# Expert tokens gathered for two blocks at a time, with a twentieth weight buffer in the place of x

## The reference

```python
def hierarchical_moe(hx, w_rg, b_rg, w_re, b_re, w_gate, w_up, w_down):
    g_prob = jax.nn.softmax((xt @ w_rg).astype(jnp.float32) + b_rg, axis=-1)
    g_w, g_idx = lax.top_k(g_prob, 1)
    e_logits = ...                                  # the 8 experts of that group
    e_top, e_loc = lax.top_k(e_logits, EXPERT_TOPK) # EXPERT_TOPK = 2
    e_w = jax.nn.softmax(e_top, axis=-1) * g_w
    e_id = g_idx * EXPERTS_PER_GROUP + e_loc
    ...
    def run_block(args):
        xb, e = args
        return (jax.nn.silu(xb @ w_gate[e]) * (xb @ w_up[e])) @ w_down[e]
    ...
    out = jnp.zeros((t, dm), jnp.float32).at[stok].add(y_sorted * sw[:, None])
```

## Time and profile before

| | |
|---|---|
| median of 3 runs | 1036.89 us |
| the profiled execution | 1034.23 us |
| its span, first to last instruction | 1032.4 us |
| PE busy | 1014.6 us (98%) |
| DVE busy / ACT busy | 508.4 us (49%) / 408.3 us (40%) |
| moved by DMA | 327.87 MB, mean 318 GB/s |
| queue q1 (all loads by SP), share of 16 engines' span | 81.4% |

### The profile page before, as it was taken

One profiled execution on the slowest core, in us unless ns is written; L12 is line 12 of the kernel. 1 busy time (PEld: TensorE's weight loads), 2 busy tenths in 40 slices (PEclk: granted clock), 3 DMA queues, 4 the chain that ended last, 5 costly groups with the idle time before them and its releaser, 6 DMA issues.

```text
span 1032.4 us, 13668 instructions
## 1 busy us (share of the span) xinstructions
PE 1014.6 (98%) x5584; PEld 678.4 (66%) x5584; DVE 508.4 (49%) x714; ACT 408.3 (40%) x643; POOL 21.8 (2%) x42
## 2 busy tenths in 40 slices
PE   8999999999999999999999999999999999999986
PEld 6888888888999999899887544444444344444322
DVE  5677677987987755667876412112221121111112
ACT  7734544435534454474874222222222122222213
POOL 0100000010000000100000000000000000000000
PEclk9999999999999999999999999999999999999999
DMA  9987558977788854364468899999999999999995
GB/s 329 391 291 244 166 190 286 329 253 245 251 311 296 292 194 164 99 244 164 163 224 335 325 389 422 419 421 421 422 421 420 422 421 420 421 421 422 421 420 212
DMA packets 86178, 327.87 MB, mean 318 GB/s; under 512 B 5744, under 2 KB 5904, under 8 KB 61408
## 3 DMA queue, kind: packets, MB, share of 16 engines
q1 hardware_dynamic: 84912, 323.98, 81.4%
q0 software_dynamic: 1200, 2.98, 0.9%
HBM read 325.88 MB, written 1.05 MB: 317 GB/s over the span
## 4 chain that ended last, share of the span: by engine, by line
PE 51%; DMA 5%; DVE 1%; ACT 0%; issue 0%; ACTq 0%; DVEq 0%
PE bank L1028 19%; PE bank L1053 9%; PE bank L1072 3%; PE bank L995 3%; DMA es<-in_w_expert_down 3%; DMA raw<-in_w_expert_gate_up 3%; PE bank L587 2%; PE bank L590 2%; PE bank L1038 2%; PE bank L593 2%; PE bank L555 1%; PE bank L558 1%; PE bank L561 1%; PE bank L1009 1%; PE bank L1011 1%; PE bank L768 1%
## 5 line engine op out<-in xcount | busy, mean ns | idle before, releaser
L1635 DVE TENSOR_TENSOR wlo<-raw,whi 128x2048 fp32r<-128x2048 f32 x87 | 199.1, 2290 | 85.7 <-ACT whi L1130 85.4
L1130 ACT ACTIVATE whi<-raw 128x2048 fp32r<-128x2048 f32 x87 | 166.0, 1913 | 95.4 <-PE bank L561 36.6
L2277 DVE SCALAR_TENSOR_TENSOR YS<-bank,wsl,gate2q 128x512 f32<-128x512 f32 x32 | 24.1, 752 | 213.8 <-PE bank L1053 213.8
L1028 PE MATMUL bank<-es,XT 128*64 128x512 f32 x488 | 112.6, 596 | 1.0 <-DMA es<-in_w_expert_gate_up 0.7
L555 PE MATMUL bank<-whi,hh 128*128 128x512 f32 x224 | 88.1, 393 | 1.2 <-ACT whi L1137 1.2
L558 PE MATMUL bank<-wlo,hh 128*128 128x512 f32 x224 | 87.3, 390 | 0.2 <-DVE wlo L1644 0.2
L561 PE MATMUL bank<-whi,hl 128*128 128x512 f32 x224 | 87.3, 390 | 0.0
L1028 PE MATMUL bank<-raw,XT 128*64 128x512 f32 x336 | 77.6, 596 | 0.4 <-DMA raw<-in_w_expert_gate_up 0.4
L1028 PEld LDWEIGHTS bank<-es,XT 128*64 128x64 f32 x488 | 33.5, 137 | 66.4 <-issue 66.1
L1624 DVE SCALAR_TENSOR_TENSOR ada_acc<-raw,silu_c,ada_acc 128x512 f32<-128x512 f32 x96 | 72.0, 750 | 2.5
L590 PE MATMUL bank<-fl,whi 128*128 128x256 f32 x256 | 72.5, 283 | 0.4 <-DVE fl L1822 0.4
(11 more groups left out here) (387 smaller groups left out, 1807.9 us busy)
## 6 DMA issues: line engine op xcount, KB each, us to landing
es<-in_w_expert_gate_up SPq DMA_DIRECT2D x61, 1024.0 KB, 24.5
raw<-in_w_expert_gate_up SPq DMA_DIRECT2D x42, 1024.0 KB, 21.1
raw<-in_w_in SPq DMA_DIRECT2D x41, 1024.0 KB, 6.0
raw<-in_w_ff SPq DMA_DIRECT2D x32, 1024.0 KB, 5.3
es<-in_w_expert_down SPq DMA_DIRECT2D x30, 1024.0 KB, 22.2
raw<-in_w_ada SPq DMA_DIRECT2D x24, 1024.0 KB, 5.7
raw<-in_w_expert_down SPq DMA_DIRECT2D x19, 1024.0 KB, 24.8
e_wlo<-in_w_expert_gate_up SPq DMA_DIRECT2D x13, 1024.0 KB, 23.0
```

The costliest lines, as they stand in the source:

```text
L1028: m = e.matmul(b[64 * w:64 * w + 64, :], K.XT[j // 4 % 2][:, k, j % 4, :], K.weights(i)[:, o:o + 512], start=k == 0, stop=k == 7)
L1130: e.activation(whi[n % RING][:, :], raw[h.raw][:, :], ACT.Copy).then_inc(S["hi"], 1)
L1635: e.tensor_tensor(wlo[n % RING][:, :], raw[h.raw][:, :], whi[n % RING][:, :].bitcast(F32), ALU.subtract).then_inc(S["lo"], 1)
```

## The change

`XT` is made for two experts at a time instead of four, 8 chunks x 2 x 64 slots, and both buffers now fit in slot 3 (4 KiB each). `gather(p, q)` covers four chunks with 128 moving columns: 16 matmuls instead of 8, two gathers per group of two experts. `PP` is half as wide. `turn_p(p)` turns two experts at once, with 128 slots stationary and the weights' matmul 2 columns wide, at even blocks only; `PT` has four buffers. ACT copies the upper four chunks of `XT`, DVE the lower four. The first block's gathers stand ahead of its matmuls, none between them. The low-part buffer `HL` of the last block is one instead of two. Slot 0 holds x until `keep_x` has read it and `th` and `tl` are written; then it is the twentieth weight buffer, last in the list, with piece 19. Later pieces go to buffer i mod 20.

```diff
-        self.XT = [slot(f"XT{k}", (3, 0)[k], [128, 8, 4, SLOTS]) for k in range(2)]
+        self.XT = [slot(f"XT{k}", 3, [128, 8, 2, SLOTS], F32, 4096 * k) for k in range(2)]
...
-        self.PP = [slot("PP0", 11, [128, 2, 4, SLOTS], F32R, 2048), slot("PP1", 1, [128, 2, 4, SLOTS], F32R, 6144)]
+        self.PP = [slot("PP0", 11, [128, 2, 2, SLOTS], F32R, 2048), slot("PP1", 1, [128, 2, 2, SLOTS], F32R, 7168)]
...
-        self.PT = [slot(f"PT{k}", 1, [128, 256], F32R, 3072 + 1024 * k) for k in range(3)]
+        self.PT = [slot(f"PT{k}", 1, [128, 256], F32R, 3072 + 1024 * k) for k in range(4)]
...
+        buffer(slot("es0", 0, [128, 2048]), "l_x1", 16, ("kept", 1), ("th", 2), ("tl", 2))
...
-            for c in range(2):
-                o = 128 * (2 * q + c)
+            for c in range(4):
+                o = 128 * (4 * q + c)
                 for i, (src, t) in enumerate(((K.th, 0), (K.th, 1), (K.tl, 0), (K.tl, 1))):
-                    m = e.matmul(b[:, 256 * c:256 * c + 256].rearrange("p (x s) -> p x s", x=4), src[:, t, o:o + 128],
+                    m = e.matmul(b[:, 128 * c:128 * c + 128].rearrange("p (x s) -> p x s", x=2), src[:, t, o:o + 128],
                                  K.PP[p % 2][:, t, :, :], start=i == 0, stop=i == 3, skip_group_check=True)
             m.then_inc(S["gat"], 1)
 
-        def turn_p(j):
+        def turn_p(p):
...
-            Pm = [K.PP[k][:, t, j % 4, :].bitcast(F32) for t in range(2)]
+            Pm = [K.PP[p % 2][:, t, :, :].rearrange("p x s -> p (x s)").bitcast(F32) for t in range(2)]
             for t in range(2):
-                e.transpose(b[0:64, 128 * t:128 * t + 128], Pm[t], C("ident"))
+                e.transpose(b[:, 128 * t:128 * t + 128], Pm[t], C("ident"))
             for t in range(2):
-                m = e.matmul(b[0:64, 256:257], Pm[t], weight(t, j - base), start=t == 0, stop=t == 1)
+                m = e.matmul(b[:, 256:258], Pm[t], weight(t, 2 * p - base), start=t == 0, stop=t == 1)
             m.then_inc(S["turnP"], 1)
...
-        gather(base // 4, 0)
-        gather(base // 4, 1)
-        gate_up(base, 0, lambda q: gather(base // 4, q + 2))
+        gather(base // 2, 0)
+        gather(base // 2, 1)
+        gate_up(base, 0)
         gate_up(base, 1)
-        turn_p(base)
-        if base + 4 < base + n:
-            gather(base // 4 + 1, 0)
+        turn_p(base // 2)
+        gather(base // 2 + 1, 0)
         for j in range(base + 1, base + n - 1):
             gate_up(j, 0)
...
-            turn_p(j)
+            if j % 2 == 0:
+                turn_p(j // 2)
             middle(j - 1)
-            if 4 * (j // 4 + 1) < base + n:
-                gather(j // 4 + 1, j % 4)
+            if 2 * (j // 2 + 1) < base + n:
+                gather(j // 2 + 1, j % 2)
             if j > base + 1:
                 combine(j - 2)
             gate_up(j, 1)
             down(j - 1)
         j = base + n - 1
         gate_up(j, 0)
-        turn_p(j)
         middle(j - 1)
...
+            for i in range(2):
+                k, own = (2 * p + i) % 4, slice(64 * i, 64 * i + 64)
+                for r in (slice(0, 64), slice(64, 128)):
+                    e.activation(K.PT[k][r, :], b[own, 0:256], ACT.Copy).then_inc(S["pt"], 1)
+                for r in (slice(0, 64), slice(64, 128)):
+                    e.activation(K.wsl[r, k:k + 1], b[own, 256 + i:257 + i], ACT.Copy).then_inc(S["pt"], 1)
...
+        def gathered(p):
+
+            e.wait_ge(S["gat"], 2 * p + 2)
+            if p > 1:
+                e.wait_ge(S["eused"], K.piece_of[2 * p - 3, "gu", 3] + 1)
+            for c in range(4):
+                k = 4 + c
                 e.activation(K.XT[p % 2][:, k, :, :],
-                             K.at[f"gat{p}_{q}"][0][:, 256 * c:256 * c + 256].rearrange("p (x s) -> p x s", x=4),
+                             K.at[f"gat{p}_1"][0][:, 128 * c:128 * c + 128].rearrange("p (x s) -> p x s", x=2),
...
             for t in range(2):
-                src = rank[:, t, 4 * p - base:4 * p - base + 4].unsqueeze(2).broadcast_to([128, 4, SLOTS])
-                e.tensor_tensor(K.PP[p % 2][:, t, :, :], io4, src, ALU.is_equal).then_inc(S["PP"], 1)
+                src = rank[:, t, 2 * p - base:2 * p - base + 2].unsqueeze(2).broadcast_to([128, 2, SLOTS])
+                e.tensor_tensor(K.PP[p % 2][:, t, :, :], io2, src, ALU.is_equal).then_inc(S["PP"], 1)
```

More of the change, by code:

```diff
@@ L347, in hidden @@
     def hidden(self, j):
-        return self.HL[(j // 4 + 1) % 2] if j in (NE - 1, NE + NOV - 1) else self.HT
+        return self.HL if j in (NE - 1, NE + NOV - 1) else self.HT
     def parted(self, j):
@@ L483, in block_uses @@
         def block_uses(base, n):
-            p0 = base // 4
-            for q in range(4):
-                use(f"gat{p0}_{q}", ((1, 2, 3, 1)[q], f"xt{q % 2}", 4 * p0 + q // 2 * 2 + 2))
+            p0 = base // 2
+            for q in range(2):
+                use(f"gat{p0}_{q}", (1 + q, f"xt{q}", 4 * p0 + 4))
             for j in range(base, base + n + 1):
-                p, q = j // 4 + 1, j % 4
+                p, q = j // 2 + 1, j % 2
                 if j < base + n:
@@ L492, in block_uses @@
                     use("over", (2, "count", 1))
-                if j < base + n:
-                    use(f"turn{j}", (3, "pt", 4 * j + 4))
+                if j < base + n and q == 0:
+                    use(f"turn{j // 2}", (3, "pt", 4 * j + 8))
                 if j > base:
                     use(f"hid{j - 1}", (2, "hf", j))
-                if j < base + n and 4 * p < base + n:
-                    use(f"gat{p}_{q}", ((j + 1) % 2 if j > base else 2, f"xt{q % 2}", 4 * p + q // 2 * 2 + 2))
+                if 2 * p < base + n:
+                    use(f"gat{p}_{q}", ((j + 1) % 2 if j > base else 2, f"xt{q}", 4 * p + 4))
                 if j > base:
@@ L1027, in gate_up @@
                         o = 1024 * w + 512 * c
-                        m = e.matmul(b[64 * w:64 * w + 64, :], K.XT[j // 4 % 2][:, k, j % 4, :],
+                        m = e.matmul(b[64 * w:64 * w + 64, :], K.XT[j // 2 % 2][:, k, j % 2, :],
                                      K.weights(i)[:, o:o + 512], start=k == 0, stop=k == 7)
                 m.then_inc(S["eused"], 1)
-                if between:
-                    between(q)
         def middle(j):
@@ L1113, in pe_program @@
     e.wait_ge(S["tl"], 2)
-    blocks(0, NE, lambda t, j: K.tab[:, 0, t, j:j + 1])
+    blocks(0, NE, lambda t, j: K.tab[:, 0, t, j:j + 2])
     e.wait_ge(S["ovf"], 1)
@@ L1118, in pe_program @@
         e.wait_ge(S["cn"], COUNTED + 89)
-        blocks(NE, NOV, lambda t, j: K.ow[:, t, j:j + 1])
+        blocks(NE, NOV, lambda t, j: K.ow[:, t, j:j + 2])
 def act_program(e, K):
@@ L1520, in blocks, with turned_p @@
     def blocks(base, n):
[L1521 to L1531, removed]
+        def turned_p(p):
+            b = K.at[f"turn{p}"][0]
+            e.wait_ge(S["turnP"], p + 1)
+            if p > 1:
+                e.wait_ge(S["comb"], 2 * p - 2)
+                e.wait_ge(S["ys"], 2 * p - 2)
+            for i in range(2):
[4 more added lines that the diff above has]
+                    e.activation(K.wsl[r, k:k + 1], b[own, 256 + i:257 + i], ACT.Copy).then_inc(S["pt"], 1)
         def gate_up(j):
@@ L1550, in down @@
             e.activation(K.YH[:, :], K.YS[:, :], ACT.Copy).then_inc(S["yh"], 1)
[L1552 to L1558, removed]
+        def gathered(p):
+            e.wait_ge(S["gat"], 2 * p + 2)
+            if p > 1:
+                e.wait_ge(S["eused"], K.piece_of[2 * p - 3, "gu", 3] + 1)
+            for c in range(4):
+                k = 4 + c
                 e.activation(K.XT[p % 2][:, k, :, :],
-                             K.at[f"gat{p}_{q}"][0][:, 256 * c:256 * c + 256].rearrange("p (x s) -> p x s", x=4),
+                             K.at[f"gat{p}_1"][0][:, 128 * c:128 * c + 128].rearrange("p (x s) -> p x s", x=2),
                              ACT.Identity, scale=K.a2c[:, k:k + 1],
                              bias=K.ada_cols[:, 16 + k:17 + k]).then_inc(S["xt1"], 1)
-        gathered(base // 4, 1)
-        gathered(base // 4, 3)
+        gathered(base // 2)
+        gate_up(base)
         count = None
@@ L1572, in blocks @@
                 down(j - 2)
-            if j < base + n:
-                turned_p(j)
+            if j < base + n and j % 2 == 0:
+                turned_p(j // 2)
             if base < j:
@@ L1578, in blocks @@
                 down(j - 2)
-            if j < base + n:
-                if j % 2 and 4 * (j // 4 + 1) < base + n:
-                    gathered(j // 4 + 1, j % 4)
+            if base < j < base + n:
+                if j % 2 and j + 1 < base + n:
+                    gathered(j // 2 + 1)
                 gate_up(j)
@@ L2282, in down @@
             e.tensor_tensor(K.YL[:, :], K.YS[:, :], K.YH[:, :].bitcast(F32), ALU.subtract).then_inc(S["yl"], 1)
[L2284 to L2289, removed]
+        one_hots(base // 2)
+        if base == 0:
```

(9 more changed lines are left out.)

40 lines of the change are left out of this document (19 added, 21 removed).

## The result

The changed kernel takes 1043.75 us, the median of 5 runs (1043.17 to 1044.82), against 1036.67 for the kernel before beside it: the ratio is 1.0074, with a 95% interval from 1.0058 to 1.0090. It is slower, by about half of what was forecast, and lies 0.25 us under the range. The profiled run took 1044.11 us, span 1042.3.

What follows compares the result with a forecast made beforehand. DMA and PE were taken to share the bound, with PE setting the end after the change. Gathers +28.7, turns -9.6 and waits -3.6 gave +15.5 us, from 1036.9 to 1052.4 us in medians; range 1044 to 1060.

Steps and rivals of the forecast that it cites:

- Its mechanism: Expert stage: loads of 128 stationary columns pace the gather matmuls and PE becomes the bound; given 80%.
- the 2.5 to 7.9 us named: Weight transfers: gain from the twentieth buffer, with the last load landing that much earlier, some 18 us ahead of its use.
- the gathers: 32 gathers, each 16 matmuls at 0.115 us instead of 8 in 0.94 us: 28.7 us added (23.6 to 31.2).
- the turns: Turns of two experts at once: 0.72 us instead of 1.32, 16 pairs saving 9.6 us (8 to 10.6).
- PE's slack: Expert blocks: PE's listed waits for weights after 560 us, 3.3 us in all, absorb added work before PE sets the end.
- the step from the profiled run to the median: Whole kernel: the profiled run stood 2.7 us under the median, so 1049.7 became 1052.4 us.
- A pair of blocks: Expert stage: two blocks were to take 28.8 us after the change (2 x 13.78 + 1.2).
- waits for weights and for the first XT: PE's waits of 3.3 us for weights and 0.3 us for XT were to go: -3.6 us.
- the 81 ns: Gather matmuls by the skill page's rate: 11.4 us added, 1.8 net of turns; edge of the about-even case, 4%.
- The terms booked at nothing: XT copies out of PSUM, ACT's longer turn and the one-hots: covered, booked at zero, 0 to 3 us in the range.
- The buffer's 2.5 us: Piece 19 in the twentieth buffer fills 2.5 us of the transfer hole, worth it only if DMA set the end.
- float32's pace of 1.72 ns per column: Rival: short float32r gather matmuls take 0.22 us each, +69.4 us in all, 1106 us; chance 8%.

Runs made afterwards that it cites:

- pad64: Kernel before with one useless float32 matmul of 64 moving columns added in each of 31 blocks; median 1.3 us above the kernel before beside it.
- pad256: Kernel before with one useless float32 matmul of 256 moving columns added in each of 31 blocks; median 9.6 us above the kernel before beside it.
- split: Kernel before with only each gather matmul of 256 moving columns cut into two of 128; 1055.19 us, ratio 1.0189.
- split_seq: Kernel before with the gather matmuls cut in two, all four addends of one half ahead of the other's; 1055.07 us, ratio 1.0191.
- turn2: Kernel before with only the turns changed, two experts per turn at even blocks, four PT buffers; 1034.26 us, ratio 0.9984.
- one_xt20: Kernel before with the twentieth buffer and a single XT, gather results written into the place just used; 1032.47 us, ratio 0.9971.
- both20: Kernel before with turns two by two, single XT and the twentieth buffer, gathers four experts wide; 1031.97 us, ratio 0.9966.
- a19: Changed kernel without its twentieth buffer, 19 buffers as before; 1043.33 us, ratio to the kernel before 1.0072.

## Why the prediction was wrong in size

Its mechanism held: gather matmuls 0.112 us apart, no wait for weights, PE busy all through, the hole filled, piece 19 issued at 574.0 us, the last load early and hidden. That load lands at 1017.0 us, 1.7 us earlier than before (1018.7), or 2.5 us counted from the stage's start; this is the low end of the 2.5 to 7.9 us named, and it is 12 us ahead of its use and not 18. What failed is the size of four terms: the gathers were priced 3.8 us too high, the turns 2.0 too low in what they save, PE's slack 1.0 too small, and the step from the profiled run to the median was booked at 2.7 us. A pair of blocks takes 28.8 us by the forecast and 28.4 by the segments of the trace. The sign was right and the kernel is 0.7% slower, not 1.5%. The terms:

| term of the sum, us | forecast | measured |
|---|---|---|
| 32 gathers | +28.7 | +24.9 |
| turns, with the transposes behind them | -9.6 | -11.6 |
| waits for weights and for the first XT | -3.6 | -4.6 |
| stage | +15.5 | +8.7 |
| outside the stage, profiled runs | 0 | +1.2 |
| from the profiled run to the median | +2.7 | -0.4 |
| from 1034.23 us to the median after | +18.2 | +9.5 |

- **The gathers.** The term was 3.8 us too high, in two parts of about the same size. The choice of 0.115 us between 0.105 and 0.120 is one: the mean over the inner matmuls of the gathers is 0.112, which over 512 of them is 1.7 us less. The other was not seen at all. The sum took the passage into and out of a gather as unchanged, but the first and the last matmul of a gather, each from its start to the next one's, took 0.41 us together before and take 0.35 after, 1.7 us less over 32 gathers. The last 0.4 us is the old pace, 0.119 us by the same mean and not 0.118. I leaned to the float32r row with 256 columns, although the row of the float32 loads with 36 columns, 0.111, was the one where the load alone sets the distance. The 0.105 us of the transposes was no low end for a load either: it is a mean over the whole passage, with a first step of 0.165 us, two of 0.109 and one of 0.028 to the gather behind them. In a matmul of 256 columns 0.118 is the pace of the moving side, and says nothing about the load under it. The Trainium skill, TensorE: Matmul & The Clock Gate, section LDWEIGHTS, gives columns / 1.2 GHz, 107 ns, and the trace agrees within 5 ns; the 81 ns of its section Back-to-back issue gap show nowhere here. By 0.107 my sum would have given 24.7 us, close to the 24.9 measured, but by luck: by the measured 0.112 it gives about 27, since it leaves out the shorter passage.
- **The turns.** I priced a turn of two at 0.72 us with an allowance for passage that isn't there. It takes 0.64 us; this is 1.3 us of the 2.0. The transposes of the hidden values give the other 0.7, a term that I had at nothing: behind a turn of two they take 0.39 us instead of 0.41, and in two blocks more a gather follows them, before which they are 0.17 us shorter than before a combine.
- **The slack.** I took the 3.3 us from the list of waits. That list counts from the modelled end of the last matmul, which lies about 0.2 us behind the point at which the next could have started. The rows show it in the kernel before; a piece takes 1.72 us from start to start when nothing waits (980.08 to 981.80), and 2.20, 2.60 and 2.38 us over the next three:

```profile
980.08 1.89 PE L1028 MATMUL bank<-es,XT 128*64 128x512 f32 x8
981.80 1.89 PE L1053 MATMUL bank<-es,SG 128*64 128x512 f32 x8
984.00 1.94 PE L1053 MATMUL bank<-es,SG 128*64 128x512 f32 x8 [0.32 <-DMA es<-in_w_expert_down]
986.60 1.94 PE L1028 MATMUL bank<-es,XT 128*64 128x512 f32 x8 [0.66 <-DMA es<-in_w_expert_gate_up]
988.98 1.94 PE L1028 MATMUL bank<-raw,XT 128*64 128x512 f32 x8 [0.44 <-DMA raw<-in_w_expert_gate_up]
```

  The three stalls are 0.48, 0.88 and 0.66 us, and listed as 0.32, 0.66 and 0.44. Both padded kernels give 4.3 us in all, already less the 0.6 that come back as the wait for YL.
- **From profile to median.** I added the 2.7 us by which the profiled run of before lay under the median of 3 runs. Against 18 and 15 later runs it is 1.9 and 1.7 us. Of that some 0.9 us is the earlier start of the stage, which goes with the clock near 437 us and not with the kernel (two runs of `pad64` with a mean clock of 0.997 took 1036.0 and 1036.5 us, the other nine 1037.2 to 1038.7). Another 1.0 us fits a shorter stage in the profiled run of before than in its ordinary ones, since against it the median grew by less than the stage in every kernel: by 1.0 to 1.6 us where PE sets the end (`pad64` 1.3 for 2.5, `pad256` 9.6 for 10.6, `split` 19.0 and `split_seq` 19.2 for 20.4, the change 7.1 for 8.7), and by 0.6 to 1.4 in `turn2`, `one_xt20` and `both20`. Ordinary runs leave no trace, so this part is inferred; more time in waits for weights would do it. The changed kernel's profiled run has a mean clock of 0.994 and lies 0.4 us over its median. The rest is spread of single runs: 3.4 us over 18 runs of before.
- **The range.** Its lower end was built from 0.105 and the largest saving on turns, +9.4, less 2 us for good measure, but with the offset of 2.7 inside. Without the offset the same sum would have put the forecast at 1049.7, still 6 us over, and the range would have held the result.
- **The terms booked at nothing** stayed there: the copies of XT, ACT's longer turn and the one-hots made no wait. The one wait that is new, 0.6 us for YL, was in no term. The buffer's 2.5 us was right as a price and rightly not in the sum, as `a19` and `one_xt20` show.

## What to carry to other kernels

Splitting a matmul by its moving side keeps the columns and doubles the loads; with 128 stationary columns, 256 moving ones of float32r are about the width at which the load (0.112 us, against 0.119 for the matmul) is still hidden, and each half of it costs nearly as much as the whole. Where two chains end together, take the slack of each from distances between starts and not from a list of idle time, and expect gains on the other one to vanish: here 10.9 us of work saved on PE were worth about 1 us of the stage, and a missing piece of transfers cost nothing once PE set the end. What freed the buffer here (half-wide gathers, 24.9 us) cost more than ten times what the buffer gives (2.3 us); writing each result into the place just used freed it at no cost to PE.

## What the runs showed of the hardware

- The stage repeated to about 10 ns in each of two pairs of kernels that PE bounds: 457.010 and 457.013 us in the changed kernel and `a19`, 468.708 and 468.719 in the two split kernels, with transfers that differ.
- A float32r matmul of 128 moving columns does not fall to float32's pace of 1.72 ns per column: it takes the time of its load, 0.111 us.
- Two float32r matmuls in a row on the same stationary piece pay for two loads, as `split` and `split_seq` show with 61.23 us of gathers each.
- A float32 load in a turn takes 0.058 us from start to start for 64 stationary columns (before) and 0.112 us for 128 (after), with 1 and 2 moving columns over it.
- The same work ahead of the stage took 0.6 to 1.3 us longer in the profiled runs in which the clock granted to TensorE stayed at 0.50 for longer after 437 us, whatever the kernel.
